# The adaptive-norm sums of two later stages: from one VectorE operation a step to a ScalarE multiply and a GpSimd add

## The chip, the cores and the metric

The kernel runs on one core of a Trainium2 chip. The metric is the device time of one launch in microseconds. "Before" was timed three times. All durations below that are not such a time come from one profiled execution.

## What is computed

Two transformer blocks stand one after the other, for 256 tokens of width 2048 in float32. The second block has two layers, each with adaptive modulation:

```python
c_act = jax.nn.silu(c)
for l in range(DEPTH_2):
    mod = c_act @ w_ada[l] + b_ada[l]                 # 2048 -> 3 * 2048
    shift, scale, gate = jnp.split(mod, 3, axis=-1)
    h = _rmsnorm(x, norm_g[l]) * (1.0 + scale[:, None, :]) + shift[:, None, :]
    z = h @ w_in[l]                                   # 2048 -> 13 pieces of 512
    ...                                               # four mixers
    y = jnp.concatenate([o_fft, o_na, o_ret, o_cv], axis=-1) @ w_out[l]
    x = x + gate[:, None, :] * y
```

The change is about `c_act @ w_ada[l]`: a product of one vector with 2 x 2048 x 6144 weights, 100 MB in all.

## The kernel before

**Blocks of the large products.** Every large weight matrix arrives in blocks of 128 x 2048 float32 (1 MB) in one of four rooms of `raw`. For each block ScalarE writes a float16 upper part (`w_hi`, L642), VectorE the float16 rest (`w_lo`, L1285), and TensorE does 48 matmuls of 256 columns (`product`, L2220). `w_hi` and `w_lo` have two slots each, so ScalarE can split block m only when TensorE has done block m-2, VectorE follows ScalarE, and TensorE starts block m when both are there and block m-1 is done. "Block m" is always the m-th of its stage. The stages of the second part are `z0` (52 blocks, from about 1251 us of the span to 1580), `mix0` (16 blocks, to about 1672), `z1` (52) and `mix1` (16).

**The modulation.** The sum `c_act @ w_ada` is cut into 12 units of 1024 outputs, and each unit into 16 steps, one for each chunk of 128 inputs. A step loads 128 x 1024 float32 of `w_ada` (0.5 MB) into one of two stage buffers (step n into buffer n % 2). VectorE multiplies it by a column of `SM` (one number a partition) and adds it to the unit's sum in one `scalar_tensor_tensor` (`ada_step`, L1256). The first step of a unit writes the sum with a `tensor_scalar` (L1253). When a unit is summed, ScalarE and VectorE split the sum in float16 parts (`ada_high`, `ada_low`), TensorE sums over the partitions (`ada_columns`, 16 matmuls of one column), and VectorE adds the bias (`ada_add`). Each of these waits for the one before it.

**What sets the order.** `ada_plan()` gives each step a stage and a block number. VectorE does the steps of block m right after its split of block m (`modulation`). The SyncE queue issues the loads: the steps of block m stand behind the weights of block m+2 (`load_due(2)`), and a step's load waits until its buffer is free, which is until step n-2 is done (`ada_used`). What stands behind a waiting load on that queue waits too. In `z0` and `z1` the old plan puts 32 steps (units 7, 8 and 10, 11) on blocks 2 to 29, three steps on two blocks up to block 10 and then one a block. In `mix0` it puts the 16 steps of unit 9 on blocks 2 to 11.

**Other VectorE work of `z0` and `z1`** stands behind the steps of its block: two `XT` updates a block (L1961) in the first blocks of `z0`, the gating of the convolution's input in block 10 (L1978, L1980), then 4 and more convolution taps a block (L1988, `TAPS_AT`) in blocks 11 to 38, and from block 20 on neighbourhood attention and rotation. GpSimd does nothing in these stages but one DMA a layer. In `mix0` VectorE adds gated results to `XT` (L2166).

Of the kernel before, what the change touches and what calls it, by code (L numbers as in the profile page):

```python
# [10 lines left out]
ALU = mybir.AluOpType  # L11
ACT = mybir.ActivationFunctionType
# [131 lines left out]
def ada_plan():  # L144

    at, count = {}, [0]

    def put(ph, m):
        at.setdefault(ph, {}).setdefault(m, []).append(count[0])
        count[0] += 1  # L150
    short = [2, 2, 3, 3, *range(4, 16)]
    def fast(ph):
        for m in [2 + 2 * k // 3 for k in range(13)] + list(range(11, 30)):
            put(ph, m)
    for m in [2 + 2 * k // 3 for k in range(16)]:
        put("w_in", m)
    for m in [3, 4, 4, 5, 6, 8, 10, 10, 12, 14, 15]:
        put("w_out", m)
    for m in [2, 2, 5, 5, 6, 6, 7, 8, 8, 10, 11, 14, 15]:
        put("wk", m)  # L160
    for ph in ("wq", "wv"):
        for k in range(26):
            put(ph, 16 * k // 26)
    for m in [0, 0, 1, 1, 2, 3, 4, 4, 5, 6, 6, 7, 8, 8, 9, 10, 10, 11, 12, 13]:
        put("wo", m)
    fast("z0")
    for m in [2, 2, 3, 4, 4, 5, 6, 6, 7, 8, 8, 9, 9, 10, 10, 11]:
        put("mix0", m)
    fast("z1")
    assert count[0] == 12 * ADA_STEPS  # L170
    return at


def ada_parts():

    names, out = {n: m for n, m, _ in STREAM}, {}
    following = {"wv": "wo"}
    for ph, steps in ada_plan().items():
        for m, ns in steps.items():
# [17 lines left out]
def build(nc, A, table, const_at, columns, router, out):  # L197
    ctx = ExitStack()
    with ctx:
# [174 lines left out]
        def ada_bank(u):  # L374
            return MB[:, 0, 0:8] if u in (8, 11) else GB[:, 2, 0:8]

# [177 lines left out]
        def _(gp):  # L554
# [64 lines left out]
        def _(act):  # L619
# [441 lines left out]
            for l in range(LAYERS):  # L1061
# [101 lines left out]
                for m in range(4 * PIECES):  # L1163
# [70 lines left out]
        def _(dve):  # L1234
# [23 lines left out]
            def ada_add(u):  # L1258
                dve.wait_ge(ada_mm, u + 1)
                mod = MOD[:, u // 6, u % 6 * 8:u % 6 * 8 + 8]  # L1260
                if u % 6 < 4:
# [4 lines left out]
            adds = {("w_in", 22): 0, ("wk", 10): 1, ("wq", 9): 2, ("wv", 3): 3, ("wv", 13): 4, ("wo", 8): 5,  # L1266
                    ("z0", 20): 7, ("z0", 33): 8, ("mix0", 14): 9, ("z1", 20): 10, ("z1", 33): 11}

# [30 lines left out]
            def modulation(ph, m):  # L1299
                if (ph, m) in parts_due:  # L1300
                    ada_low(parts_due[ph, m])
                for n in plan.get(ph, {}).get(m, []):
                    ada_step(n)
                if (ph, m) in adds:
# [660 lines left out]
            for l in range(LAYERS):  # L1965
# [202 lines left out]
                for m in range(2, 16):  # L2168
# [5 lines left out]
                    for p in nth(m, 6, 2, 5):  # L2174
                        pair_add(mix, p + 1)
                    if l == 0 and m == 14:
                        dve.wait_ge(ada_mod, 10)
# [22 lines left out]
        def _(pe):  # L2200
# [472 lines left out]
            for l in range(LAYERS):  # L2673
# [44 lines left out]
                def ret_scores(c):  # L2718
                    if c == 0:
                        pe.wait_ge(S("rotated"), 4 * l + 4)  # L2720
                        pe.wait_ge(S("na_max"), 8 * l + 8)
                        pe.wait_ge(ada_mod, 9 + 3 * l)
                    else:
# [100 lines left out]
                for m in range(4 * PIECES):  # L2824
                    if l == 0 and m == 3:
                        spread_root(3, r_first)
                    if m == 17:
                        ada_columns(7 + 3 * l)
                    if m == 32:
                        pe.wait_ge(S("na_max"), 8 * l + 8)  # L2830
                        ada_columns(8 + 3 * l)
# [31 lines left out]
                for m in range(16):  # L2863
                    if l == 0 and m == 13:
                        ada_columns(9)
# [107 lines left out]
```

## Time and profile before

| what | us |
|---|---|
| median of three runs (lowest, highest) | 2107.47 (2106.94, 2107.79) |
| time of the profiled execution | 2106.58 |
| its span | 2104.8 |
| TensorE busy in it | 2051.7 (97%) |
| VectorE busy | 1748.3 (83%) |
| ScalarE busy | 1195.1 (57%) |
| GpSimd busy | 41.3 (2%) |

The kernel is read as a row of stages in which TensorE hardly ever stops. The span less TensorE's busy time is 53 us, 28 us of it before 1251 us. What matters for a change in the later stages is where TensorE waits there and what it waits for.

### The profile page before, as it was taken

How to read it: one execution, taken by the hardware profiler on the slowest of the kernel's cores; microseconds unless marked ns; L12 is line 12 of the kernel's file. 1: busy time of each engine (PE TensorE's matmuls, PEld its weight loads, DVE VectorE, ACT ScalarE, POOL GpSimd, SP SyncE). 2: the span in 40 equal slices, each digit the busy share in tenths (PEclk: the TensorE clock that was granted, in tenths of full speed). 3: DMA queues.
4: the chain of work that ended last, by engine and by line, in shares of the span. 5: the costliest groups of instructions: out<-in, count | busy, mean ns of one | idle time of the engine just before them, and what ended most of it. 6: DMA issues, size and time to landing. Idle time of an engine off the chain costs nothing.

```text
span 2104.8 us, 42665 instructions
## 1 busy us (share of the span) xinstructions
PE 2051.7 (97%) x19032; PEld 1655.8 (79%) x19032; DVE 1748.3 (83%) x1660; ACT 1195.1 (57%) x1069; POOL 41.3 (2%) x40
## 2 busy tenths in 40 slices
PE   8999999999999999999999999999999999999998
PEld 7889888888889946555555568888888788888887
DVE  7885787988887798999999998999568789995655
ACT  5554644444434577887878864356554443565543
POOL 0002300000000000000000000000000000000000
PEclk9999999999999999999999999999999999999999
DMA  7854487788888878999999977874458778744552
GB/s 299 319 200 161 167 318 266 285 314 319 312 321 308 299 282 341 420 421 420 421 420 414 405 296 288 296 257 161 143 178 302 281 298 301 252 166 142 180 200 101
DMA packets 95718, 593.25 MB, mean 282 GB/s; under 512 B 10664, under 2 KB 10824, under 8 KB 36784
## 3 DMA queue, kind: packets, MB, share of 16 engines
q1 hardware_dynamic: 94912, 583.73, 74.0%
q0 software_dynamic: 624, 6.80, 0.8%
q8 instruction: 150, 2.46, 0.5%
q14 instruction: 32, 0.26, 0.0%
HBM read 588.39 MB, written 2.10 MB: 281 GB/s over the span
## 4 chain that ended last, share of the span: by engine, by line
PE 66%; DVE 17%; DMA 11%; ACT 3%; issue 3%; SPq 0%; DVEq 0%; POOL 0%; ACTq 0%; POOLq 0%
PE GB L2220 50%; DVE w_lo L1285 6%; DMA W<-w_ada 4%; PE GB L2646 4%; DVE W L1285 4%; PE MB L2646 3%; DMA Z<-w_ada 2%; ACT w_hi L642 2%; DMA raw<-w_down 2%; DVE W L1256 1%; DVE Z L1256 1%; DMA raw<-w_gate 1%; DMA raw<-w_up 1%; DMA Z<-w_up 1%; PE MB L2818 1%
## 5 line engine op out<-in xcount | busy, mean ns | idle before, releaser
L642 ACT ACTIVATE w_hi<-raw 128x2048 f16<-128x2048 f32 x294 | 561.2, 1910 | 710.4 <-PE GB L2220 687.8
L1285 DVE SCALAR_TENSOR_TENSOR w_lo<-raw,w_hi 128x2048 f16<-128x2048 f32 x294 | 674.1, 2294 | 245.9 <-ACT w_hi L642 244.8
L2220 PE MATMUL GB<-H,w_hi 128*128 128x256 f16 x4352 | 717.4, 273 | 18.2 <-DVE w_lo L1285 12.2
L2220 PE MATMUL GB<-H,w_lo 128*128 128x256 f16 x2176 | 593.2, 273 | 0.0
L2220 PEld LDWEIGHTS GB<-H,w_hi 128*128 128x128 f16 x4352 | 421.4, 98 | 84.0 <-DVE w_lo L1285 16.6
L2220 PEld LDWEIGHTS GB<-H,w_lo 128*128 128x128 f16 x2176 | 213.0, 98 | 24.7
L2220 PE MATMUL GB<-w_hi,H 128*128 128x256 f16 x1280 | 210.8, 273 | 0.9 <-DVE w_lo L1285 0.9
L1256 DVE SCALAR_TENSOR_TENSOR W<-W,SM 128x1024 f32<-128x1024 f32 x120 | 153.8, 1282 | 36.1 <-DMA W<-w_ada 32.8
L2220 PE MATMUL GB<-w_lo,H 128*128 128x256 f16 x640 | 174.4, 273 | 0.0
L2220 PE MATMUL GB<-Z,w_hi 128*128 128x256 f16 x1024 | 170.0, 274 | 3.6 <-DVE w_lo L1285 3.6
L2220 PE MATMUL GB<-W,w_hi 128*128 128x256 f16 x1024 | 168.0, 273 | 2.1 <-DVE w_lo L1285 2.1
L1285 DVE SCALAR_TENSOR_TENSOR W<-raw,W 128x2048 f16<-128x2048 f32 x68 | 154.4, 2286 | 3.4 <-ACT W L642 3.2
L642 ACT ACTIVATE W<-raw 128x2048 f16<-128x2048 f32 x68 | 129.6, 1912 | 30.4 <-PE GB L2646 8.1
L2220 PE MATMUL GB<-Z,w_lo 128*128 128x256 f16 x512 | 140.3, 274 | 0.0
L2220 PE MATMUL GB<-W,w_lo 128*128 128x256 f16 x512 | 139.6, 273 | 0.0
L2220 PEld LDWEIGHTS GB<-w_hi,H 128*128 128x128 f16 x1280 | 124.6, 98 | 17.4 <-DVE w_lo L1285 1.8
L2220 PEld LDWEIGHTS GB<-Z,w_hi 128*128 128x128 f16 x1024 | 100.3, 98 | 16.7 <-DVE w_lo L1285 4.5
L2220 PEld LDWEIGHTS GB<-W,w_hi 128*128 128x128 f16 x1024 | 99.9, 98 | 14.1 <-DVE w_lo L1285 2.6
L1988 DVE SCALAR_TENSOR_TENSOR Y<-Y,PC 128x256 f32<-128x256 f32 x240 | 99.6, 478 | 0.0
L2646 PE MATMUL MB<-W,Z 128*64 (+1 forms) x864 | 85.9, 353 | 3.5 <-DVE W L1285 2.0
L2646 PE MATMUL GB<-W,Z 128*64 (+1 forms) x864 | 86.5, 353 | 2.0 <-ACT Z L974 1.7
L2646 PE MATMUL GB<-w_hi,Z 128*64 (+1 forms) x576 | 84.8, 359 | 2.6 <-DVE Z L1858 1.5
(485 smaller groups left out, 2806.9 us busy)
## 6 DMA issues: line engine op xcount, KB each, us to landing
raw<-w_in SPq DMA_DIRECT2D x144, 1024.0 KB, 5.0
W<-w_ada SPq DMA_DIRECT2D x128, 512.0 KB, 5.6
raw<-w_out SPq DMA_DIRECT2D x48, 1024.0 KB, 5.2
raw<-w_down SPq DMA_DIRECT2D x41, 1024.0 KB, 10.7
raw<-w_gate SPq DMA_DIRECT2D x34, 1024.0 KB, 10.2
raw<-w_up SPq DMA_DIRECT2D x32, 1024.0 KB, 11.9
Z<-w_ada SPq DMA_DIRECT2D x64, 512.0 KB, 6.0
raw<-xattn_wk SPq DMA_DIRECT2D x16, 1024.0 KB, 5.2
```

What stands on the lines that cost most here:

```text
L642: act.activation(w, raw_at[r], ACT.Copy, scale=W_SCALE).then_inc(hi_done, 1)
L1256: dve.scalar_tensor_tensor(sums, w, SM[:, 24 + k:25 + k], sums, ALU.mult, ALU.add).then_inc(ada_used[n % 2], 1)
L1285: dve.scalar_tensor_tensor(lo, raw_at[r], W_SCALE, hi, ALU.mult, ALU.subtract).then_inc(raw_taken[r], 1)
L1988: dve.scalar_tensor_tensor(ca[:, c, :], CU[:, c, k // 4:k // 4 + T], col("conv_w_2", l * TAPS * 4 + k), ca[:, c, :], ALU.mult, ALU.add).th ...
L2220: last = pe.matmul(o, a, m, start=first, stop=end and w_part is lo, skip_group_check=True)
L2646: ins = pe.matmul(o_bank(j, k)[r:r + SLOT], x[:, c0 + c, at_:at_ + SLOT], v, start=kh == 0 and c == 0 and part == 0, stop=kh == 7 and c == ...
L2818: ins = pe.matmul(banks[:, n // 2, n % 2 * T:n % 2 * T + T], w[:, k, n * P:n * P + P], x[:, k, :], start=n % 2 == 0 and k == 0, stop=k == ...
```

## The change

The steps of `z0`, `mix0` and `z1` (80 of the 192) leave VectorE. ScalarE multiplies the arrived weights in place (`ada_scaled`), behind its split of the block and the copies out of PSUM; the first step of a unit writes the sum itself and needs no add. GpSimd adds the other 75 to the sum and frees the buffer (`ada_step` in the GpSimd program). The steps of `z0` and `z1` now stand on blocks 3 to 33: `3, 4, 4, 5, 6, ... 33`. Those of `mix0` stay on blocks 2 to 11, one of them a block later. The splits of the sums, the column sums and the bias adds move to later blocks to match, and the column sums of units 8 and 11 go to another PSUM bank.

```diff
+ON_GPSIMD = ("z0", "mix0", "z1")
-    def fast(ph):
-        for m in [2 + 2 * k // 3 for k in range(13)] + list(range(11, 30)):
+    def steady(ph):
+        for m in [3, 4] + list(range(4, 34)):
             put(ph, m)
-    for m in [2, 2, 3, 4, 4, 5, 6, 6, 7, 8, 8, 9, 9, 10, 10, 11]:
+    for m in [2, 2, 3, 4, 4, 5, 6, 6, 7, 8, 8, 9, 10, 10, 11, 11]:
         put("mix0", m)
...
+            def ada_step(n):
+                if n % ADA_STEPS == 0:
+                    return
+                gp.wait_ge(S("ada_scaled"), n - 7 * ADA_STEPS - (n // ADA_STEPS - 7))
+                gp.wait_ge(ada_used[(n - 1) % 2], (n - 1) // 2 + 1)
+                sums = ada_sums(n // ADA_STEPS)
+                gp.tensor_tensor(sums, sums, ada_stage(n), ALU.add).then_inc(ada_used[n % 2], 1)
...
+            def ada_scaled(ph, m):
+                for n in plan.get(ph, {}).get(m, []):
+                    u, k = n // ADA_STEPS, n % ADA_STEPS
+                    act.wait_ge(ada_full[n % 2], 16 * (n // 2 + 1))
+                    c, w = SM[:, 24 + k:25 + k], ada_stage(n)
+                    if k:
+                        act.activation(w, w, ACT.Copy, scale=c).then_inc(S("ada_scaled"), 1)
+                        continue
+                    act.wait_ge(ada_mm, u - 1)
+                    act.activation(ada_sums(u), w, ACT.Copy, scale=c).then_inc(ada_used[n % 2], 1)
...
-                    ("z0", 20): 7, ("z0", 33): 8, ("mix0", 14): 9, ("z1", 20): 10, ("z1", 33): 11}
+                    ("z0", 24): 7, ("z0", 40): 8, ("mix0", 15): 9, ("z1", 24): 10, ("z1", 40): 11}
...
-                for n in plan.get(ph, {}).get(m, []):
-                    ada_step(n)
+                if ph not in ON_GPSIMD:
+                    for n in plan.get(ph, {}).get(m, []):
+                        ada_step(n)
...
-                        pe.wait_ge(ada_mod, 9 + 3 * l)
...
                 def conv_sum(k, src, o):
                     if k == 0:
+                        pe.wait_ge(ada_mod, 9 + 3 * l)
...
-                    if m == 17:
+                    if m == 22:
                         ada_columns(7 + 3 * l)
-                    if m == 32:
-                        pe.wait_ge(S("na_max"), 8 * l + 8)
+                    if m == 37:
+                        pe.wait_ge(S("rotated"), 4 * l + 4)
                         ada_columns(8 + 3 * l)
```

On VectorE, in blocks 11 to 13 of `z0`, the steps stand between the split and the taps before:

```order
L1285 SCALAR_TENSOR_TENSOR w_lo<-raw,w_hi 128x2048 [waits hi_done]
L1256 SCALAR_TENSOR_TENSOR Z<-Z,SM 128x1024 [waits ada_used1,ada_full0]
L1988 SCALAR_TENSOR_TENSOR Y<-Y,PC 128x256 [waits tap] x4
L1285 SCALAR_TENSOR_TENSOR w_lo<-raw,w_hi 128x2048 [waits hi_done]
L1256 SCALAR_TENSOR_TENSOR Z<-Z,SM 128x1024 [waits ada_used0,ada_full1]
L1988 SCALAR_TENSOR_TENSOR Y<-Y,PC 128x256 [waits tap] x4
```

Now, with line numbers of the changed kernel, only split and taps are left:

```order
L1312 SCALAR_TENSOR_TENSOR w_lo<-raw,w_hi 128x2048 [waits hi_done]
L2016 SCALAR_TENSOR_TENSOR Y<-Y,PC 128x256 [waits tap] x4
L1312 SCALAR_TENSOR_TENSOR w_lo<-raw,w_hi 128x2048 [waits hi_done]
L2016 SCALAR_TENSOR_TENSOR Y<-Y,PC 128x256 [waits tap] x4
L1312 SCALAR_TENSOR_TENSOR w_lo<-raw,w_hi 128x2048 [waits hi_done]
```

One VectorE operation of each block is gone, and with it VectorE's wait for the arrival of `w_ada`.

On ScalarE, in blocks 4 to 7 of `mix0`, there were splits (L642) and the squares of a pair of `XT` chunks (L932):

```order
L642 ACTIVATE w_hi<-raw 128x2048 [waits block_done0,raw_full2]
L932 ACTIVATE Z<-XT 128x512 [waits bank_free0]
L642 ACTIVATE w_hi<-raw 128x2048 [waits block_done1,raw_full3]
L642 ACTIVATE w_hi<-raw 128x2048 [waits block_done0,raw_full0]
L932 ACTIVATE Z<-XT 128x512 [waits bank_free1]
L642 ACTIVATE w_hi<-raw 128x2048 [waits block_done1,raw_full1]
```

Now the multiplies (L672) stand between them, each with its wait for the load (`ada_full`):

```order
L655 ACTIVATE w_hi<-raw 128x2048 [waits block_done0,raw_full2]
L672 ACTIVATE W<-W,SM 128x1024 [waits ada_full1]
L672 ACTIVATE W<-W,SM 128x1024 [waits ada_full0]
L956 ACTIVATE Z<-XT 128x512 [waits bank_free0]
L655 ACTIVATE w_hi<-raw 128x2048 [waits block_done1,raw_full3]
L672 ACTIVATE W<-W,SM 128x1024 [waits ada_full1]
L655 ACTIVATE w_hi<-raw 128x2048 [waits block_done0,raw_full0]
L672 ACTIVATE W<-W,SM 128x1024 [waits ada_full0]
L672 ACTIVATE W<-W,SM 128x1024 [waits ada_full1]
```

Six multiplies moved in front of the splits of blocks 5 to 8, and the wait for `w_ada` came with them.

## Rows read from the trace of the kernel before

**Rows 1.** Page, part 1: busy us (share of the span) and instructions.

```profile
PE 2051.7 (97%) x19032; PEld 1655.8 (79%) x19032; DVE 1748.3 (83%) x1660; ACT 1195.1 (57%) x1069; POOL 41.3 (2%) x40
```

**Rows 2.** Windows: stretch, us, then busy us (instructions) of each engine, clock, DMA.

```profile
1268.00:1345.00 77.00, 73.00 (x660) 63.98 (x658) 71.12 (x80) 32.15 (x23) 0.00 (x0) 1.00 0.85 309
1345.00:1543.00 198.00, 196.70 (x1715) 165.38 (x1714) 167.48 (x216) 113.22 (x142) 0.00 (x0) 1.00 0.57 196
...
1625.00:1672.00 47.00, 44.76 (x420) 39.44 (x418) 35.39 (x33) 20.36 (x16) 0.00 (x0) 1.00 0.73 261
1695.00:1738.00 43.00, 42.19 (x387) 37.58 (x386) 34.29 (x26) 19.11 (x14) 0.00 (x0) 1.00 0.95 360
1738.00:1783.00 45.00, 43.85 (x415) 39.12 (x413) 44.17 (x53) 18.17 (x13) 0.00 (x0) 1.00 0.84 298
1783.00:1872.00 89.00, 88.23 (x784) 74.26 (x783) 88.28 (x130) 53.94 (x84) 0.00 (x0) 1.00 0.63 220
```

**Rows 3.** Waits of TensorE in mix0 and z0: start, length, operation, [idle before].

```profile
1638.49 0.39 PE L2220 MATMUL GB<-W,w_hi 128*128 128x256 f16 x2 [1.20 <-DVE w_lo L1285]
...
1318.74 0.39 PE L2220 MATMUL GB<-H,w_hi 128*128 128x256 f16 x2 [1.40 <-DVE w_lo L1285]
```

**Rows 4.** Timeline of VectorE in z1, blocks 10 to 13.

```profile
1734.72 1.28 DVE L1256 SCALAR_TENSOR_TENSOR Z<-Z,SM 128x1024 f32<-128x1024 f32 x1 [1.12 <-DMA Z<-w_ada]
...
1737.26 1.38 DVE L1980 TENSOR_SCALAR Y<-Y,PC 128x256 f32<-128x256 f32 x4
...
1743.54 2.29 DVE L1285 SCALAR_TENSOR_TENSOR w_lo<-raw,w_hi 128x2048 f16<-128x2048 f32 x1
1745.74 1.28 DVE L1256 SCALAR_TENSOR_TENSOR Z<-Z,SM 128x1024 f32<-128x1024 f32 x1
1746.94 1.67 DVE L1988 SCALAR_TENSOR_TENSOR Y<-Y,PC 128x256 f32<-128x256 f32 x4
1748.52 2.28 DVE L1285 SCALAR_TENSOR_TENSOR w_lo<-raw,w_hi 128x2048 f16<-128x2048 f32 x1
```

**Rows 5.** Timeline of ScalarE in z1 and mix0.

```profile
1746.41 1.91 ACT L642 ACTIVATE w_hi<-raw 128x2048 f16<-128x2048 f32 x1 [4.65 <-PE GB L2220]
...
1751.65 1.91 ACT L642 ACTIVATE w_hi<-raw 128x2048 f16<-128x2048 f32 x1 [2.85 <-PE GB L2220]
...
1646.01 1.06 ACT L651 ACTIVATE ada_hi<-W 128x1024 f16<-128x1024 f32 x1
```

**Rows 6.** Timeline of GpSimd from 188 us, where it works beside VectorE.

```profile
188.38 1.88 POOL L580 TENSOR_TENSOR Z<-Z 128x1020 f32<-128x1020 f32 x1
...
192.37 1.44 POOL L591 TENSOR_TENSOR Y<-Z 128x512 f32<-128x512 f32 x1
...
214.25 3.92 POOL L580 TENSOR_TENSOR Y<-Z 128x1016 f32<-128x1016 f32 x1
```

**Rows 7.** Timeline of VectorE in the same stretch.

```profile
188.48 2.07 DVE L1511 TENSOR_TENSOR Z<-Z,RT 128x256 f32<-128x256 f32 x1
...
191.93 0.41 DVE L1511 TENSOR_TENSOR Z<-Z,RT 128x256 f32<-128x256 f32 x1
...
192.60 3.35 DVE L1285 SCALAR_TENSOR_TENSOR w_lo<-raw,w_hi 128x2048 f16<-128x2048 f32 x1
...
214.16 2.28 DVE L1285 SCALAR_TENSOR_TENSOR w_lo<-raw,w_hi 128x2048 f16<-128x2048 f32 x1
```

**Rows 8.** Timelines of VectorE and GpSimd at the end of the span.

```profile
2096.53 3.55 DVE L2196 TENSOR_TENSOR Z<-XT,MB 128x1024 f32<-128x1024 f32 x4 [1.29 <-PE MB L2272]
...
2097.36 2.35 POOL L615 TENSOR_TENSOR Z<-XT,NS 128x1024 f32<-128x1024 f32 x1 [422.18 <-ACT NS L1230]
```

**Rows 9.** DMA issues from 1590 to 1650 us, and of the page: KB, median us to landing.

```profile
W<-w_ada SPq DMA_DIRECT2D x14, 512.0 KB, 4.8
...
Z<-w_ada SPq DMA_DIRECT2D x64, 512.0 KB, 6.0
```

**Rows 10.** Chain that ended last, a piece of z1: start, us, what.

```profile
1721.17 3.92 DMA Z<-w_ada
```

More of the change, by code:

```diff
@@ L165, in ada_plan @@
         put("wo", m)
-    fast("z0")
-    for m in [2, 2, 3, 4, 4, 5, 6, 6, 7, 8, 8, 9, 9, 10, 10, 11]:
+    steady("z0")
+    for m in [2, 2, 3, 4, 4, 5, 6, 6, 7, 8, 8, 9, 10, 10, 11, 11]:
         put("mix0", m)
-    fast("z1")
+    steady("z1")
     assert count[0] == 12 * ADA_STEPS
@@ L181, in ada_parts @@
                 if n % ADA_STEPS == ADA_STEPS - 1:
+                    m += ph in ON_GPSIMD
                     out[(ph, m + 1) if m + 1 < names[ph] else (following[ph], 0)] = n // ADA_STEPS
@@ L374, in ada_bank @@
         def ada_bank(u):
-            return MB[:, 0, 0:8] if u in (8, 11) else GB[:, 2, 0:8]
+            return GB[:, 2, 0:8]
         def na_p(h):
@@ L613, in _ @@
                 gp.dma_start(W[:, 0:2 * BLK], A["na_rel_bias_2"][l]).then_inc(S("bias_in"), 16)
+                for ph in (f"z{l}", f"mix{l}"):
+                    for n in [n for m in sorted(plan.get(ph, {})) for n in plan[ph][m]]:
+                        ada_step(n)
             gp.wait_ge(S("final_x"), 8)
@@ L1169, in _ @@
                         evict(i, 1)
+                    if m >= 3:
+                        ada_scaled(ph, m)
                     for c in nth(m, 22, 3):
@@ L1213, in _ @@
                     split(mix, m)
+                    ada_scaled(mix, m)
                     for p in nth(m, 4, 2, 6):
@@ L1301, in modulation @@
                     ada_low(parts_due[ph, m])
-                for n in plan.get(ph, {}).get(m, []):
-                    ada_step(n)
+                if ph not in ON_GPSIMD:
+                    for n in plan.get(ph, {}).get(m, []):
+                        ada_step(n)
                 if (ph, m) in adds:
@@ L2175, in _ @@
                         pair_add(mix, p + 1)
-                    if l == 0 and m == 14:
+                    if l == 0 and m == 15:
                         dve.wait_ge(ada_mod, 10)
@@ L2863, in _ @@
                 for m in range(16):
-                    if l == 0 and m == 13:
+                    if l == 0 and m == 14:
                         ada_columns(9)
```

## The prediction

> **What bounds the kernel now.** I read the page's busy shares first: TensorE is busy 97% of the span and VectorE 83% [rows 1]. A change off TensorE can only give back TensorE's waits, or add to them. So the second view is the windows over the stages that the change touches [rows 2]: TensorE idles 4.00 us of 1268 to 1345 and 1.30 of 1345 to 1543 (z0), 2.24 of 1625 to 1672 (mix0), and 0.81, 1.15 and 0.77 of the three stretches of z1. That is 10.3 us, of which some 0.9 (short gaps at small products) are not VectorE's. **At most 9.4 us can be won**, 0.45% of the time. The third view is what TensorE waits for: VectorE's split `w_lo`, 1.40 us in z0 and 1.20 in mix0 at the longest [rows 3].
>
> The fourth is how full VectorE is. In blocks 11 to 19 of z1 it is busy 44.17 of 45 us, in blocks 20 to 33 88.28 of 89 [rows 2], while TensorE hardly waits: **VectorE stands exactly at the edge there**. One block is split 2.20 (start to start), step 1.20, taps 1.58, together 4.98 us [rows 4], against 5.24 between ScalarE's splits, which is TensorE's pace (1746.41 to 1751.65) [rows 5]. The slack inside a block is 5.24 less ScalarE's 1.91, VectorE's 2.29 and handovers of 0.1, so 0.9 us.
>
> **The parts of the change: VectorE.** It sheds 75 steps of 1.20 and 5 shorter ones. What matters is how its other operations get on beside GpSimd's adds. Beside GpSimd's add of 1.88 us a VectorE operation of 0.41 took 2.07, so it stood for 1.66; a split of 2.29 took 3.35 beside an add that had begun 0.23 earlier and ended 1.21 after the split's start; and the other way round an add of the same kind took 3.92 where a split of 2.28 had begun first [rows 6, 7]. **The two exclude each other for nearly the whole instruction.** A rate shared in halves would have given other numbers. The exception is also in the trace: four VectorE operations with one operand in PSUM took 3.55 us, 1024 + 1024 + 512 + 512 columns at the usual rate, while GpSimd worked [rows 8]. The split, the taps and the rotation have both inputs in SBUF; the `XT` updates and the masks of attention have one in PSUM.
>
> A rule that speaks against the change is in the Trainium skill, "GPSIMD Engine Reference", section "Engine selection": elementwise adds belong on VectorE. The Trainium skill's same page, section "Elementwise — side-by-side cycle accounting", has 4497 ns for an add of 2048 columns on GpSimd, from which I estimate 2.25 us for 1024. The trace has 1.88 us for 1020 columns [rows 6]; by the Trainium skill's figure the sum would be some 5 to 10 us larger, which is near rival (c).
>
> So a step costs VectorE 0 before the add and up to 1.75 us with it (1.88 less its last 0.13 to 0.15, in which VectorE already ran: 1.06 of 1.21), in place of 1.20. **Bounds of a step for VectorE: -1.20 (the add falls wholly beside idle or PSUM work) to +0.55 (it falls beside nothing of the kind).**
>
> Blocks 11 to 19 of z have nothing but splits and taps: 3.78 + 1.75 = 5.53, with the lost overlap of two starts 5.6 us against 5.24. That is 0.36 for each of 9 blocks, 3.2 us. Block 10 holds the gating, 2.5 us between the end of its step and the next split, and its step waits 1.12 us for the load [rows 4]. It goes to 2.2 + 2.5 + 1.75 = 6.45 of 5.24, and the 1.2 above it less the slack of 0.9 cost 0.4. Together 3.6. Against the 1.15 us that z1 loses there now [rows 2], this is **+2.4**; in z0, which loses 1.40 there [rows 3], **+2.2**.
>
> Blocks 20 to 33: VectorE's 88.28 us less ten steps (12.0) and a split of the sums that moves on to block 35 (1.1) is 75.1. Fourteen adds bring 24.5, so 99.6, of which four adds can lie beside the attention's masks and maxima (7.0) and some beside copies out of PSUM (3.1): 89.5 against 89. I take +0.5 for this, +0.5 for ScalarE below, each in z0 and z1; bounds -0.8 and +10.
>
> The first blocks of z: VectorE no longer waits for loads ahead of a split. Of the 2.6 us lost there in z0 (4.00 - 1.40) and 0.8 in z1, 0.8 stays in z0 (block 5 waits for its load on ScalarE, and the next split comes late). **-1.8 and -0.8.**
>
> **ScalarE** gets 80 multiplies of about 1.0 us (the nearest row is 1.06 for 1024 columns with another output type [rows 5]). Cover: it waits 2.85 us before a split in block 12 [rows 5], and is busy 53.94 of 89 us in blocks 20 to 33 [rows 2]; with 14 us more, 68 of 89. Only block 22 with its exponentials overruns. What it costs when the cover is gone: everything behind a late multiply on ScalarE, which is the next split, and so TensorE.
>
> **The loads in mix0** are the largest term. A buffer goes round like this: load 4.8 us [rows 9], multiply 1.0, add 1.9, handovers 0.1, so 7.8; with two buffers 3.9 us a step. Before it was 4.8 + 1.28, so 3.05 a step. The plan wants 16 steps in blocks 2 to 11, 1.6 a block, so 3.3 us a step. Before, the ring just held and lost 2.1 us; now a block cannot be faster than 1.6 x 3.9 = 6.2 us. Walking it block by block (split, multiplies as their loads land, next split not before them; adds behind VectorE's splits, 2.25 us at most) gives waits of TensorE of 1.5, 2.2, 2.0, 2.0 and 2.1 at blocks 5, 7, 9, 11 and 12, together 9.8. **+7.7.** With landings of 3.9, the shortest on the chain that ended last [rows 10], seven rounds give back 6.3; with 6.0, the median over z0 and z1 [rows 9], they cost 8.4 more: **bounds +1.4 and +16**. I take 4.8, since it is the row of this stage. On SyncE's queue the weight loads stand behind those of the steps; they are issued three blocks ahead, which covers waits of 2 us.
>
> In z with one step a block the ring has 10.5 us a round and needs 6.0 + 1.0 + 1.9 and up to 2.3 behind a split, 11.2 at worst: ScalarE waits some tenths, in cover. TensorE's waits on the column sums and biases come 3 and more blocks after the last step: nothing.
>
> **Sum.** z0: -1.8 + 2.2 + 1.0 = +1.4. z1: -0.8 + 2.4 + 1.0 = +2.6. mix0: +7.7. Together +11.7 on a span of 2104.8: 2116.5. The profiled execution was 1.8 us above its span and 0.9 below the median, so the median comes to **2119.2 us**.
>
> **Rivals.** (a) Faster, 2101.5: the exclusion decides. If VectorE's splits and taps are not held up by adds (GpSimd gives way, or its adds fall into VectorE's idle time, as the operations of 0.41 beside GpSimd's one-input work did (at 191.93) [rows 7]), all of z's waits of 7.3 us (4.6 and 2.7) come back; with landings of 3.9 mix0 costs 1.4, together -5.9. It decides at 0.26 us of held time a block, VectorE's room in blocks 11 to 19. Against it: rows 6 and 7. (b) No change, 2107 to 2111: one of the two mechanisms is absent. With no exclusion and the ring as walked: -7.3 + 7.7, 2108. With landings of 3.9 and half of z's 4.0: +3.4, 2111. (c) Worse, 2135: the add takes 2.35 us as the only one of 1024 columns did [rows 8], which is 0.47 x 23 blocks x 2 in z less some overlap (+14), and 3 us in mix0; ScalarE then waits for loads in blocks 20 to 33 with little cover. (d) The steps of mix0 are not spread by the change; a reader of its title would expect them to be. That is in the sum.
>
> **How the numbers follow.** Forecast 0.48, (c) 0.19, (b) 0.18, (a) 0.15. A measurement can tell about 0.2%, 4.2 us. Slower is the forecast, (c) and 0.03 of (b): 0.70. Within 0.2% is the rest of (b) and 0.02 of (a): 0.17. Faster: 0.13. The range leaves out (a) and the far end of (c): 2103 to 2137.
>
> **What would show it.** Right: TensorE's idle time in mix0 near 10 us with ScalarE's next split late behind a wait for `w_ada`; splits of VectorE of 3 to 4 us in blocks 11 to 33; VectorE still some 95% busy in z1's blocks 11 to 19. Wrong: splits of 2.29 throughout, adds under 1.5 us, or landings under 4 us in mix0. If the splits are long and TensorE doesn't wait, then the room in blocks 11 to 33 was larger than I read it.

## The result and the profile after

The changed kernel takes 2147.61 us (median of four runs, 2144.84 to 2150.33) against 2107.20 of the kernel before in the same comparison: ratio 1.0191, interval 1.0178 to 1.0205, so 40.4 us slower. The forecast was 12 us slower with a range up to 2137. The sign was right, the size was a third of what came, and the time lies outside the range.

The profiled execution is the longest of the four: 2150.33 us, span 2148.5, so 43.7 more than the span before (2104.8). What its stages show is therefore some 3 us more than the medians do.

Busy time of the engines, to be read beside [rows 1]:

```profile
PE 2063.3 (96%) x19032; PEld 1659.3 (77%) x19032; DVE 1749.0 (81%) x1580; ACT 1279.1 (60%) x1149; POOL 268.8 (13%) x115
```

Two lines tell most of the story. VectorE has 80 instructions less, and is busy as long as before (1749.0 against 1748.3). TensorE does the same 19032 matmuls in 11.6 us more, and idles 32.1 us more (2148.5 less 2063.3 against 2104.8 less 2051.7).

The stages, cut at the starts of ScalarE's splits of blocks 3, 11, 20 and 34 of `z0`, 0 of `mix0`, 2, 11, 20 and 34 of `z1`, and 0 of `mix1`. The windows view of the changed kernel (columns as in [rows 2]):

```profile
1266.10:1309.80 43.70, 42.07 (x382) 37.15 (x381) 27.70 (x29) 28.32 (x23) 21.15 (x8) 1.00 0.81 291
1309.80:1365.70 55.90, 49.41 (x435) 42.73 (x433) 52.20 (x49) 30.08 (x25) 25.59 (x9) 0.97 0.73 260
1365.70:1461.00 95.30, 90.46 (x783) 74.98 (x781) 93.34 (x112) 67.36 (x98) 50.74 (x15) 0.98 0.64 227
1461.00:1593.20 132.20, 128.27 (x1084) 108.77 (x1084) 89.88 (x91) 66.92 (x66) 0.00 (x0) 1.00 0.47 160
1593.20:1708.70 115.50, 103.87 (x917) 90.16 (x915) 73.03 (x79) 65.47 (x63) 38.44 (x16) 0.97 0.75 269
1708.70:1758.20 49.50, 47.45 (x434) 42.04 (x433) 28.05 (x22) 31.75 (x28) 21.33 (x8) 1.00 0.73 265
1758.20:1811.90 53.70, 47.68 (x435) 41.97 (x433) 52.21 (x47) 30.26 (x24) 27.37 (x9) 1.00 0.75 266
1811.90:1914.00 102.10, 92.74 (x784) 75.76 (x781) 100.99 (x116) 67.84 (x98) 41.77 (x15) 0.97 0.60 212
1914.00:2044.80 130.80, 128.17 (x1084) 108.68 (x1084) 88.65 (x89) 66.89 (x66) 1.58 (x1) 1.00 0.47 162
```

And of the kernel before, blocks 20 to 33 of `z0` and of `z1`, cut in the same way:

```profile
1362.00:1450.80 88.80, 88.23 (x782) 74.18 (x781) 88.15 (x129) 53.95 (x85) 0.00 (x0) 1.00 0.63 221
1783.50:1872.50 89.00, 88.23 (x783) 74.21 (x781) 88.28 (x131) 53.96 (x85) 0.00 (x0) 1.00 0.63 220
```

The lengths beside those of before, and beside four of the kernels below, each cut in the same way from its own trace (us):

| stage | before | after | predicted more | came more | step_on_vector | add_on_vector | tail_on_vector | mix0_alone |
|---|---|---|---|---|---|---|---|---|
| z0, blocks 3 to 10 | 44.1 | 43.7 | -1.8 | -0.4 | 41.8 | 42.5 | 41.7 | 41.7 |
| z0, 11 to 19 | 50.2 | 55.9 | +2.2 | +5.7 | 48.7 | 48.6 | 48.7 | 48.7 |
| z0, 20 to 33 | 88.8 | 95.3 | +1.0 | +6.5 | 90.2 | 89.4 | 88.4 | 88.4 |
| z0, 34 to the end | 129.0 | 132.2 | 0 | +3.2 | 133.0 | 132.9 | 130.2 | 130.2 |
| mix0 to block 2 of z1 | 106.7 | 115.5 | +7.7 | +8.8 | 107.6 | 111.2 | 107.2 | 114.0 |
| z1, 2 to 10 | 48.1 | 49.5 | -0.8 | +1.4 | 47.1 | 48.0 | 47.1 | 47.2 |
| z1, 11 to 19 | 48.9 | 53.7 | +2.4 | +4.8 | 47.3 | 47.2 | 47.3 | 47.3 |
| z1, 20 to 33 | 89.0 | 102.1 | +1.0 | +13.1 | 90.5 | 89.6 | 88.4 | 88.3 |
| z1, 34 to the end | 129.0 | 130.8 | 0 | +1.8 | 131.3 | 131.2 | 130.2 | 130.2 |

The parts of `z0` are 15.0 us longer, `mix0` 8.8, the parts of `z1` 21.1.

**Where VectorE's gain went.** The groups of VectorE's taps and splits, of GpSimd's adds and of ScalarE's multiplies, as in part 5 of the page (busy us, mean ns of one | idle before):

```profile
L2016 DVE SCALAR_TENSOR_TENSOR Y<-Y,PC 128x256 f32<-128x256 f32 x240 | 170.8, 772 | 0.0
L1312 DVE SCALAR_TENSOR_TENSOR w_lo<-raw,w_hi 128x2048 f16<-128x2048 f32 x294 | 683.8, 2327 | 306.0 <-ACT w_hi L655 304.7 <-DVE Y L2016 0.3
L578 POOL TENSOR_TENSOR Z<-Z 128x1024 f32<-128x1024 f32 x60 | 189.5, 3159 | 243.9 <-ACT Z L672 243.6
L578 POOL TENSOR_TENSOR W<-W 128x1024 f32<-128x1024 f32 x15 | 37.9, 2525 | 171.3 <-ACT W L672 171.2
L672 ACT ACTIVATE Z<-Z,SM 128x1024 f32<-128x1024 f32 x60 | 68.4, 1140 | 11.7 <-DMA Z<-w_ada 11.6
```

Before, the 294 splits were busy 674.1 us, and the 240 taps:

```profile
L1988 DVE SCALAR_TENSOR_TENSOR Y<-Y,PC 128x256 f32<-128x256 f32 x240 | 99.6, 478 | 0.0
```

So the taps alone took back 71.2 us and the splits 9.7. A timeline of VectorE in blocks 11 and on of `z0`:

```profile
1316.58 4.97 DVE L2016 SCALAR_TENSOR_TENSOR Y<-Y,PC 128x256 f32<-128x256 f32 x4
1321.48 2.28 DVE L1312 SCALAR_TENSOR_TENSOR w_lo<-raw,w_hi 128x2048 f16<-128x2048 f32 x1
1323.68 3.78 DVE L2016 SCALAR_TENSOR_TENSOR Y<-Y,PC 128x256 f32<-128x256 f32 x4
1327.38 2.28 DVE L1312 SCALAR_TENSOR_TENSOR w_lo<-raw,w_hi 128x2048 f16<-128x2048 f32 x1
1329.59 1.66 DVE L2016 SCALAR_TENSOR_TENSOR Y<-Y,PC 128x256 f32<-128x256 f32 x4
...
1344.53 2.27 DVE L1312 SCALAR_TENSOR_TENSOR w_lo<-raw,w_hi 128x2048 f16<-128x2048 f32 x1
1346.73 5.91 DVE L2016 SCALAR_TENSOR_TENSOR Y<-Y,PC 128x256 f32<-128x256 f32 x4
1352.57 2.28 DVE L1312 SCALAR_TENSOR_TENSOR w_lo<-raw,w_hi 128x2048 f16<-128x2048 f32 x1
```

And GpSimd's in the same stretch:

```profile
1324.84 2.34 POOL L578 TENSOR_TENSOR Z<-Z 128x1024 f32<-128x1024 f32 x1 [3.96 <-ACT Z L672]
...
1344.30 4.73 POOL L578 TENSOR_TENSOR Z<-Z 128x1024 f32<-128x1024 f32 x1 [1.17 <-ACT Z L672]
1350.02 2.35 POOL L578 TENSOR_TENSOR Z<-Z 128x1024 f32<-128x1024 f32 x1 [0.99 <-ACT Z L672]
```

Four taps take 1.66 us without an add, 3.78 with one (2.12 more, of an add of 2.34), and 5.91 where two adds fall on them. The first of the two had begun beside the split and itself took 4.73. A block with one add goes from split to split in 5.90 us (1321.48 to 1327.38), where TensorE needs 5.24. With two adds it is 8.04 (1344.53 to 1352.57), and the short blocks beside it can give back little, since the weights' parts have two slots only. The hold fell on the taps and hardly on the splits (mean 2327 ns, 2294 before), so the prediction's sign for it, splits of 3 to 4 us, was the wrong place to look.

**What some waits cost on top.** Timeline of TensorE at the same place:

```profile
1323.81 0.61 PE L2248 MATMUL GB<-H,w_hi 128*128 128x256 f16 x2 [2.58 <-DVE w_lo L1312]
```

The windows view ahead of its start and behind it:

```profile
1320.00:1324.00 4.00, 1.42 (x13) 0.99 (x11) 4.00 (x4) 2.67 (x3) 0.88 (x1) 0.93 0.38 140
1324.00:1327.00 3.00, 3.00 (x16) 2.17 (x15) 3.00 (x4) 0.76 (x1) 2.16 (x1) 0.52 0.70 238
1327.00:1330.50 3.50, 3.50 (x34) 3.14 (x33) 3.50 (x5) 0.00 (x0) 0.18 (x1) 1.00 0.60 246
```

Behind a wait of 2.58 us the granted clock is 0.52, the lower level of 1.2 GHz, and TensorE does 16 matmuls in 3.00 us in place of about 30. Not every wait is followed by this. The same kernel's wait of 2.63 us that ends at 1354.9 is not:

```profile
1354.00:1358.00 4.00, 3.09 (x29) 2.78 (x30) 4.00 (x6) 1.32 (x2) 0.00 (x0) 1.00 0.55 150
```

Of its seven waits of 2 us or more in these nine stages two are followed by the lower clock, and so are three of 1.77 to 1.97 us. Over the span the mean granted clock is 0.987 against 0.992. That is 2148.5 x 0.013 less 2104.8 x 0.008, 11.1 us, beside the 11.6 us by which the same matmuls were busy longer. Not all of it belongs to the change: in the nine stages TensorE is busy 10.1 us longer, and the clocks and lengths of their windows give some 8 us.

**mix0.** ScalarE ahead of its split of block 7 of `mix0`, with its waits for the loads:

```profile
1629.90 1.15 ACT L672 ACTIVATE W<-W,SM 128x1024 f32<-128x1024 f32 x1 [2.60 <-DMA W<-w_ada]
1633.38 1.15 ACT L672 ACTIVATE W<-W,SM 128x1024 f32<-128x1024 f32 x1 [2.33 <-DMA W<-w_ada]
1634.44 0.61 ACT L956 ACTIVATE Z<-XT 128x512 f32<-128x512 f32 x1
1634.96 1.89 ACT L655 ACTIVATE w_hi<-raw 128x2048 f16<-128x2048 f32 x1
```

TensorE's longest wait there:

```profile
1639.78 0.39 PE L2248 MATMUL GB<-W,w_hi 128*128 128x256 f16 x2 [3.79 <-DVE w_lo L1312]
```

The split comes late behind two waits for `w_ada`, as the walk had it. A hold adds to it: an operation of VectorE that takes 0.68 us alone takes 2.43 beside GpSimd's add, and VectorE begins its split 0.6 us after ScalarE has done its own:

```profile
1635.08 2.43 DVE L1365 TENSOR_TENSOR Z<-Z 128x512 f32<-128x512 f32 x1 [5.00 <-ACT Z L956]
```

### The profile page after: what moved, and what is told of

Its sections match the earlier page's. It is cut to its first block, busy times and chain, and to the rows that moved or that the text cites. A ratio compares the mean times of both kernels' runs of the same rounds, so it can differ in the third digit from the quotient of the medians.

```text
span 2148.5 us, 42741 instructions
## 1 busy us (share of the span) xinstructions
PE 2063.3 (96%) x19032; PEld 1659.3 (77%) x19032; DVE 1749.0 (81%) x1580; ACT 1279.1 (60%) x1149; POOL 268.8 (13%) x115
## 3 DMA queue, kind: packets, MB, share of 16 engines
q8 instruction: 150, 2.46, 0.4%
## 4 chain that ended last, share of the span: by engine, by line
PE 52%; DVE 20%; issue 13%; DMA 8%; ACT 5%; POOL 1%; POOLq 0%; ACTq 0%; SPq 0%; DVEq 0%
PE GB L2248 38%; DVE w_lo L1312 8%; PE GB L2674 4%; DVE Y L2016 4%; DVE W L1312 3%; PE MB L2674 3%; ACT w_hi L655 3%; DMA W<-w_ada 3%; DMA raw<-w_up 2%; DMA raw<-w_down 1%; POOL W L578 1%; DMA raw<-w_gate 1%; DMA Z<-w_up 1%; DMA Z<-w_down 1%; DVE W L1283 1%
## 5 line engine op out<-in xcount | busy, mean ns | idle before, releaser
L1312 DVE SCALAR_TENSOR_TENSOR w_lo<-raw,w_hi 128x2048 f16<-128x2048 f32 x294 | 683.8, 2327 | 306.0 <-ACT w_hi L655 304.7
L2248 PE MATMUL GB<-H,w_hi 128*128 128x256 f16 x4352 | 725.1, 274 | 30.9 <-DVE w_lo L1312 26.2
L578 POOL TENSOR_TENSOR Z<-Z 128x1024 f32<-128x1024 f32 x60 | 189.5, 3159 | 243.9 <-ACT Z L672 243.6
L2016 DVE SCALAR_TENSOR_TENSOR Y<-Y,PC 128x256 f32<-128x256 f32 x240 | 170.8, 772 | 0.0
L1283 DVE SCALAR_TENSOR_TENSOR W<-W,SM 128x1024 f32<-128x1024 f32 x105 | 134.6, 1282 | 19.9 <-DMA W<-w_ada 16.8
```

The lines of the kernel that those rows point to most:

```text
L578: gp.tensor_tensor(sums, sums, ada_stage(n), ALU.add).then_inc(ada_used[n % 2], 1)
L1283: dve.scalar_tensor_tensor(sums, w, SM[:, 24 + k:25 + k], sums, ALU.mult, ALU.add).then_inc(ada_used[n % 2], 1)
L1312: dve.scalar_tensor_tensor(lo, raw_at[r], W_SCALE, hi, ALU.mult, ALU.subtract).then_inc(raw_taken[r], 1)
L2016: dve.scalar_tensor_tensor(ca[:, c, :], CU[:, c, k // 4:k // 4 + T], col("conv_w_2", l * TAPS * 4 + k), ca[:, c, :], ALU.mult, ALU.add).th ...
L2248: last = pe.matmul(o, a, m, start=first, stop=end and w_part is lo, skip_group_check=True)
```

## The experiments

The theory before the runs, H: VectorE stands still while GpSimd adds, and this is what costs in `z0` and `z1`. Rivals: S, that the cost is the extra ScalarE work and the longer use of the two stage buffers; P, that it is the new plan of blocks. Beside the kernels before and after, ten more stand in the table. "z" is the sum of the eight stages of `z0` and `z1` above, "mix0" that stage, "taps" the mean ns of one of the 240 taps. The kernel before was 2107.20 us in the comparison of the changed kernel, 2105.18 in that of the next eight and 2106.61 in that of the last two. Three of the expectations below (tail_on_vector, tail_on_gpsimd, mix0_alone) count stages from cuts one or two blocks earlier: there `mix0` is 102.4 us before, 111.3 after and 102.8 in tail_on_vector, and what the change adds behind the cut near block 34 is 9 us in both layers (5.0 in the table above).

| kernel | median us (lowest, highest) | ratio [interval] | z | mix0 | taps |
|---|---|---|---|---|---|
| before | | | 627.1 | 106.7 | 478 |
| after | 2147.61 (2144.84, 2150.33) | 1.0191 [1.0178, 1.0205] | 663.2 | 115.5 | 772 |
| add_on_vector | 2115.04 (2109.99, 2121.14) | 1.0046 [1.0029, 1.0063] | 629.4 | 111.2 | 477 |
| step_on_vector | 2109.12 (2106.83, 2115.88) | 1.0019 [1.0004, 1.0034] | 629.9 | 107.6 | 476 |
| add_64_columns | 2096.90 (2092.00, 2101.15) | 0.9954 [0.9934, 0.9973] | 619.1 | 107.4 | 482 |
| add_512_columns | 2103.84 (2101.79, 2105.86) | 0.9993 [0.9980, 1.0006] | 619.3 | 110.9 | 584 |
| one_input | 2108.71 (one run) | | 623.2 | 115.5 | 558 |
| mix0_back | 2136.01 (2132.51, 2139.37) | 1.0139 [1.0112, 1.0165] | 659.0 | 109.2 | 749 |
| tail_on_vector | 2100.95 (2098.56, 2105.97) | 0.9979 [0.9965, 0.9992] | 622.0 | 107.2 | 479 |
| tail_on_gpsimd | 2144.80 (2135.01, 2148.72) | 1.0196 [1.0166, 1.0226] | 647.6 | 115.1 | 730 |
| mix0_alone | 2109.31 (2106.21, 2113.35) | 1.0014 [1.0002, 1.0027] | 622.0 | 114.0 | 482 |
| add_in_quarters | 2148.16 (2145.45, 2152.23) | 1.0211 [1.0191, 1.0231] | 647.0 | 128.0 | 696 |

### add_on_vector: is it that GpSimd adds?

```diff
-                for ph in (f"z{l}", f"mix{l}"):
-                    for n in [n for m in sorted(plan.get(ph, {})) for n in plan[ph][m]]:
-                        ada_step(n)
...
+            def ada_sum(n):
...
+                dve.tensor_tensor(sums, sums, ada_stage(n), ALU.add).then_inc(ada_used[n % 2], 1)
...
-                if ph not in ON_GPSIMD:
-                    for n in plan.get(ph, {}).get(m, []):
-                        ada_step(n)
+                for n in plan.get(ph, {}).get(m, []):
+                    (ada_sum if ph in ON_GPSIMD else ada_step)(n)
```

> The multiply stays on ScalarE, the add of the 75 steps goes from GpSimd to VectorE (a tensor_tensor of some 1.2 us in the step's old place); plan and column sums as in the changed kernel. Theory H (GpSimd's add of 2.34 us holds VectorE's operations with two inputs in SBUF): no hold is left, VectorE needs 4.9 us a block as before, so the 36 us that z0 and z1 lost go; what stays is the longer ring of mix0 (4.8 + 1.1 + 1.2 = 7.1 us a round, 5.7 a block: +3 to +5), so 2107 to 2114. Theory S (ScalarE's multiply with its wait for the load makes the next split late): nothing changes there, 2135 or more.

1.0046, where the changed kernel is 1.0191: 1.45% or some 30 us go with GpSimd alone, though VectorE now does 75 adds more. The groups of VectorE's taps and of its new adds:

```profile
L2020 DVE SCALAR_TENSOR_TENSOR Y<-Y,PC 128x256 f32<-128x256 f32 x240 | 99.5, 477 | 0.0
L1288 DVE TENSOR_TENSOR Z<-Z 128x1024 f32<-128x1024 f32 x60 | 73.1, 1218 | 3.4 <-ACT Z L669 3.1
```

The taps are back at 477 ns with all of ScalarE's multiplies in place. An add that takes VectorE 1.22 us as its own work took it 2.12 as GpSimd's. The time, 2115.04 us, is 1 us above the range that H gave and 20 under that of S. H holds for z (629.4 us against 663.2), and S is excluded there.

### add_64_columns and add_512_columns: by length

```diff
-                gp.tensor_tensor(sums, sums, ada_stage(n), ALU.add).then_inc(ada_used[n % 2], 1)
+                gp.tensor_tensor(sums[:, 0:64], sums[:, 0:64], ada_stage(n)[:, 0:64], ALU.add).then_inc(ada_used[n % 2], 1)
```

> GpSimd adds only the first 64 of the 1024 columns of each step, so the sums of units 7 to 11 leave out most of their terms; multiplies, loads and waits are all there. Theory H: the hold shrinks from 2.3 to some 0.3 us a step, VectorE is rid of 1.2 us a step, and the ring of mix0 is down to 6.3 us a round: 2099 to 2105, faster than before. Theory S: 2135 or more.

> GpSimd adds half of each step's columns (the other half of each sum is left out), 1.27 us by the rows of 512 columns. Theory H: what the hold takes (1.1 us) is what VectorE was rid of (1.2), so the loss is not half of the way between 64 and 1024 columns (2122) but most of it is gone: 2103 to 2113. If every held microsecond costs TensorE the same, 2120 or more.

With 64 columns z is 619.1 us, 8.0 under before and 44.1 under after, and the time is 2 us below the range given. With 512 columns z is 619.3, so half an add costs nothing at all over one of 64 columns, and a whole one 43.9 us. The timeline of VectorE in two blocks of `z0` with 512 columns shows why:

```profile
1325.64 2.68 DVE L2016 SCALAR_TENSOR_TENSOR Y<-Y,PC 128x256 f32<-128x256 f32 x4
1328.68 2.29 DVE L1312 SCALAR_TENSOR_TENSOR w_lo<-raw,w_hi 128x2048 f16<-128x2048 f32 x1 [0.35 <-ACT w_hi L655]
1330.89 2.68 DVE L2016 SCALAR_TENSOR_TENSOR Y<-Y,PC 128x256 f32<-128x256 f32 x4
```

The hold is there, 1.02 us for an add of 1.35 (2.68 less 1.66), but 2.20 + 2.68 is 4.9 of TensorE's 5.24, and VectorE still waits 0.35. With 2.12 it is 5.90. **The price of a hold is what stands out of the block's slack**, here 1.46 us by this sum: a hold of 1.02 was free, one of 2.12 was not.

### one_input: does a GpSimd operation that reads one operand hold VectorE?

```diff
-                gp.tensor_tensor(sums, sums, ada_stage(n), ALU.add).then_inc(ada_used[n % 2], 1)
+                gp.tensor_scalar(sums, ada_stage(n), 1.0, None, ALU.mult).then_inc(ada_used[n % 2], 1)
```

> GpSimd copies the scaled weights over the sum with a tensor_scalar of 1024 columns instead of adding them, so each sum holds its last step alone. Question: does an operation with one input of the same size hold VectorE as the add does? If each operation of GpSimd that reads SBUF holds the pair for its whole length (some 3 us by the row of 1.49 us for 512 columns), 2150 or more. If it holds it only while it reads, less than the add: under 2130.

z is 623.2, under before; what is lost is in `mix0`. The timeline of VectorE beside such a copy in `z0`:

```profile
1334.93 2.44 DVE L2016 SCALAR_TENSOR_TENSOR Y<-Y,PC 128x256 f32<-128x256 f32 x4
```

And that of GpSimd at the same time:

```profile
1335.89 2.94 POOL L578 TENSOR_SCALAR Z<-Z 128x1024 f32<-128x1024 f32 x1 [3.49 <-ACT Z L672]
```

GpSimd is busy longer than with the add (2.94 against 2.34 at the shortest) and the taps are held 0.78 us only. VectorE's next split starts at 1337.96, while the copy still runs, and takes its usual 2.29. So it is not GpSimd's being busy that holds VectorE. The copy differs from the add in its second operand and in its kind of instruction; that the operand makes the difference is likely, and not shown apart. It is a single run; the blocks before and behind this one show the same 2.44.

### add_in_quarters: one long hold or four short ones

```diff
-                gp.tensor_tensor(sums, sums, ada_stage(n), ALU.add).then_inc(ada_used[n % 2], 1)
+                for q in range(4):
+                    cut = slice(256 * q, 256 * q + 256)
+                    ins = gp.tensor_tensor(sums[:, cut], sums[:, cut], ada_stage(n)[:, cut], ALU.add)
+                ins.then_inc(ada_used[n % 2], 1)
```

> The changed kernel with each GpSimd add of 1024 columns cut into four of 256 columns; the sums are the same. Theory T (VectorE stands still for as long as GpSimd's two-input work takes in all, however it is cut): VectorE's four taps of blocks 11 to 19 are still 3.5 to 6 us, and the time is 2143 to 2155. Theory L (a hold lasts for one instruction and VectorE gets in between two; an add of 512 columns cost nothing, so what costs is one long hold that the block's slack can't take): VectorE and GpSimd take turns, the taps beside an add take about 1.7 + 2.4 us at the most since the total is the same, but the split of ScalarE's next block is met by shorter holds, and the time is 2120 to 2143. Theory S (a short instruction hardly holds VectorE at all, its reading being the only exclusive part): the taps take under 2.5 us beside the quarters and the time is 2104 to 2115.

The time fits theory T's number and most of the reason is not T's. z falls by 16.2 us (663.2 to 647.0), and most groups of four taps take 3.3 to 3.6 us beside the quarters, where a whole add made 3.8 of them, so VectorE does get in between two instructions, as theory L had it. In blocks 11 to 19 it is held as long in all as with whole adds (busy 52.1 and 51.2 us against 52.2 and 52.2), in blocks 20 to 33 less (90.0 and 92.0 against 93.3 and 101.0). But the four instructions of a step take GpSimd longer (61.1 us for the 60 in `mix0`, 4.1 a step against 2.5), and `mix0` goes from 115.5 to 128.0. The time alone would have misled; the stages tell it.

### step_on_vector and tail_on_vector: what the new plan does

step_on_vector is the changed kernel with whole steps on VectorE, as before, but at the new blocks; ScalarE's multiplies and GpSimd's adds are gone.

```diff
...
-                if ph not in ON_GPSIMD:
-                    for n in plan.get(ph, {}).get(m, []):
-                        ada_step(n)
+                for n in plan.get(ph, {}).get(m, []):
+                    ada_step(n)
```

> Whole steps back on VectorE (the fused operation of 1.28 us), but at the new places of the plan and with the moved column sums. Theory H and theory S: 2103 to 2109, since neither the hold nor the multiply is left. Theory P (the new plan itself costs, through four more steps in the full blocks 30 to 33 and the later column sums): 2112 or more.

1.0019, and 2109.12 us, at the upper edge of the range of H and S; the 2112 or more of P did not come. The stages are worth more than the sum: the steadier plan gains 3.8 and 2.6 us up to block 20 of the two stages and loses 5.4 and 3.8 behind it, 4.0 and 2.3 of them behind block 34. TensorE at block 34 of `z0` in this kernel:

```profile
1461.61 1.14 PE L2747 MATMUL MB<-Z 64*128 64x256 f32 x8 [2.74 <-DVE Z L2044]
1462.68 0.39 PE L2241 MATMUL GB<-H,w_hi 128*128 128x256 f16 x2
...
1463.03 0.63 PE L2241 MATMUL GB<-H,w_hi 128*128 128x256 f16 x2
```

The windows view of the wait and of what follows it:

```profile
1459.00:1462.70 3.70, 1.09 (x9) 0.71 (x10) 3.63 (x7) 3.31 (x3) 0.00 (x0) 1.00 0.70 213
1463.00:1466.00 3.00, 3.00 (x16) 2.13 (x15) 3.00 (x4) 2.20 (x3) 0.00 (x0) 0.50 0.13 52
```

The retention scores wait 2.74 us for VectorE's rotation (before it does not wait for it), because steps on blocks 30 to 33 stand ahead of it on VectorE, and behind the wait the clock is 0.50 for 3 us. In `z1` the same product waits 2.74 us too, and the clock behind it stays at 1.00:

```profile
1887.00:1892.00 5.00, 4.96 (x44) 4.18 (x45) 5.00 (x7) 3.02 (x5) 0.00 (x0) 1.00 0.35 146
```

In the changed kernel the same product waits 1.55 us in `z0` and 1.75 in `z1`. With adds of 64 or 512 columns at the same blocks the product doesn't wait (under 0.5 us). So I moved the last four steps behind the rotation, and the column sums from block 37 to 39 (`mix0` has its old plan again):

```diff
-        for m in [3, 4] + list(range(4, 34)):
+        for m in [3, 4] + list(range(4, 30)) + [34, 35, 36, 37]:
...
-                    if m == 37:
+                    if m == 39:
```

> Steps on VectorE as before the change, mix0 as before. In z0 and z1 the steps stand on blocks 3, 4, 4, 5, ... 29 and 34 to 37, so one a block, but not on blocks 30 to 33, where the rotation for TensorE's products of block 34 is made; the second column sum comes at block 39. Theory R (the 4 us that step_on_vector lost at block 34 of each layer come from VectorE's late rotation): the gain of the even first blocks (4.7 us in step_on_vector's stages) stays and the loss goes, 2099 to 2103 where before is 2105. If the loss at block 34 is of the later column sums, it stays: 2108 or more.

2100.95, ratio 0.9979 [0.9965, 0.9992]: **faster than the kernel before** by 4.2 us, with the change's plan mended and no step on GpSimd. The same product waits 0.74 us, and the loss behind block 20 is down to 0.8 and 0.6 us. The column sums come later here than in step_on_vector, so they did not make its loss.

> The changed kernel (multiply on ScalarE, add on GpSimd) with the same placing, nothing on blocks 30 to 33 but four steps on 34 to 37. Theory R for the part that TensorE loses after block 33 (9 us in both layers) and theory H for the rest: 2136 to 2142. By theory H alone, with the number of adds what counts and not their place: 2146 or more.

The same plan with GpSimd's adds gave 1.0196, beside 1.0191 of the changed kernel. The time doesn't tell the two expectations apart; the runs spread over 14 us, and the profiled one is the shortest. Its blocks 20 to 33 are 2.8 and 7.4 us shorter than those of the changed kernel, with four adds fewer in them, and what follows 0.8 and 0.7. Whether this is a gain in the median stays open.

### mix0_back and mix0_alone: the two stage buffers

mix0_back takes only `mix0` back to VectorE and the old plan; mix0_alone is tail_on_vector with only `mix0` as in the change.

The line that differs in mix0_back, and the same line in mix0_alone:

```diff
-ON_GPSIMD = ("z0", "mix0", "z1")
+ON_GPSIMD = ("z0", "z1")
...
-ON_GPSIMD = ("z0", "mix0", "z1")
+ON_GPSIMD = ("mix0",)
```

> The 16 steps of mix0 stand on VectorE again with the old plan for them; z0 and z1 as in the changed kernel. If the three stages add up, what mix0 lost (8.7 us of the stage's length) comes back: 2138 to 2140. If mix0's loss was made in z0 (late splits carried over), less than 4 us come back.

> z0 and z1 as in tail_on_vector (whole steps on VectorE, none on blocks 30 to 33), and only the 16 steps of mix0 as in the change: multiplied by ScalarE, added by GpSimd, with the change's plan for mix0. Theory A (the loss in mix0 is that of the two stage buffers, which are taken longer by a multiply and an add, and is independent of z0 and z1): the stage of mix0 up to block 2 of z1 is 111 us as in the change (102.8 in tail_on_vector), all other stages are within 0.5 us of tail_on_vector, and the time is 2100.95 + 8.5, so 2107 to 2111. Rival B (much of that loss in the change is work that z0 left late, or needs adds in z1): the stage is under 107 us and the time under 2105.

Taken away, the change in `mix0` gives back 6.3 us of its stage and 0.5% of the time (1.0191 to 1.0139). Done alone, it costs 6.8 us of its stage and 0.35% (0.9979 to 1.0014), and z stays at 622.0. So most of the 8.8 us is independent of the holds in z; some 2 us come only with them. The first came out 2 us below its range and the second 1.5 us under the changed kernel's stage, which theory A had it reach; its time is in A's range.

The column "mix0" over all kernels is a second test. A buffer is taken for the load, and then for a step of: 1.28 us whole on VectorE (106.7 to 107.6, and 109.2 in mix0_back), 1.15 + 0.46 with 64 columns (107.4), 1.15 + 1.22 with the add on VectorE (111.2), 1.15 + 1.35 with 512 columns (110.9), 1.15 + 2.53 in the change (115.5), 1.15 + 2.90 with one input (115.5), 1.15 + 4.1 in quarters (128.0). The stage grows with this time, whichever engine does the step.

## Why the prediction was wrong, step by step

**The bound on what could be won, 9.4 us: right.** With the holds nearly gone (add_64_columns) z is 8.0 us shorter than before, where TensorE's waits in z had been put at 7.3, and the median 8.3.

Two small readings of the prediction are off, without effect on the sum: the wait of 2.85 us stands before ScalarE's split of block 14, not 12, and 1.2 less 0.9 is 0.3 for block 10.

**"A step costs VectorE up to 1.75 us (1.88 less its last 0.13 to 0.15)": the mechanism was right, the term was mis-sized.** The add takes 2.34 us and holds 2.12. I took the 1.88 of [rows 6], an add of a tile to a shifted view of it; the only add of two operands of 1024 columns in the trace was the 2.35 of [rows 8], which I priced as rival (c). The estimate from the Trainium skill, "GPSIMD Engine Reference", section "Elementwise — side-by-side cycle accounting", 2.25 us, was nearer than my row; the measured number is 2.34. The difference of 0.37 is small for an add, but it is all above the slack: in blocks 11 to 19 the same sum with 2.12 is 3.78 + 2.12 = 5.90 a block, 53.1 us for nine, and 53.7 came in `z1`. In `z0` 55.9 came. There block 10's gating was held, one block had two adds on its taps, and the clock was at the lower level for 3 us. With 1.75 it was 5.6, or 50.4.

**"Blocks 20 to 33: 89.5 against 89, so +0.5" (and 0.5 for ScalarE): the step that failed most**, with +6.5 and +13.1 us. Fourteen adds at 2.12 in place of 1.75 are 5.2 us of it. With them the forecast of VectorE's busy time, 1.2 us more than before, becomes 6.4 more. In `z0` 5.2 more came (93.34 against 88.15), so there the cover of 10.1 us, adds beside operations with an input in PSUM, was about right. In `z1` 12.7 more came (100.99 against 88.28), so some 6 us of that cover were not there: the same fourteen adds fell on taps. Why they fell so in one layer and not in the other the runs don't show; mix0_back has it too (92.2 and 101.9 us). The other 1.3 and 0.4 us are idle time of VectorE itself, which the sum took as none. TensorE at the lower clock, for 3 us in `z0` and twice that in `z1`, is part of these lengths too. ScalarE had room (67.36 of 95.30), as predicted.

**"Waits on column sums and biases: nothing": true of these, but the wrong wait was asked.** The steps on blocks 30 to 33 delay the rotation, and with it TensorE's scores at block 34. The stages from block 34 on are 3.2 and 1.8 us longer in the change, 4.0 and 2.3 in step_on_vector, where GpSimd adds nothing, and 1.2 each once the four steps stand behind it. I had costed the move of the steps by VectorE's total, not by who waits for the operation behind them.

**First blocks, -1.8 and -0.8: wrong, -0.4 and +1.4.** With whole steps on VectorE at the new blocks the gain was there (-2.3 and -1.0), with ScalarE's multiplies and the adds on VectorE it was -1.6 and -0.1. I had costed no hold beside the `XT` updates and the gating; a `TENSOR_TENSOR` of the gating took 2.46 us in the change and 1.16 in the two kernels without GpSimd.

**mix0, +7.7: the place and the mechanism right, the number helped by luck.** +8.8 came. TensorE waited 0.78, 3.79, 2.12 and 2.07 us in it, 8.8 together, where the walk had 9.8 in five waits. But a round of a buffer was longer than I took it: landings of 4.7 us (4.8 taken), multiplies of 1.15 (1.0) and adds of 2.53 (1.9), 0.7 us more. By the walk's own rule, 6.3 us for 0.9 a round, that is 5 us on top of 7.7. They did not come, and done alone the change in `mix0` cost 6.8. What made up for them is open.

**No term for the clock: missing.** Some 8 of the 44 us of the profiled execution are matmuls at the lower clock behind waits. I had costed each wait at its own length.

**Together:** in z the forecast was +4.0 and +36.1 came, 17.6 of the difference in blocks 20 to 33. Rival (c) had the right price for the add (2.35) and 28 us in all; it lacked the rotation, the clock and the missing cover in `z1`. I gave it 0.19 because I took the size of the add from the row whose engine neighbourhood was best, and not from the row whose shape was the same. My range ended at 2137 since it left the far end of (c) out; with my own bounds of +10 for blocks 20 to 33 of each stage and +16 for `mix0` the sum reaches 2146, which is still under what came.

## What to carry to other kernels

Moving a two-input SBUF operation from VectorE to GpSimd doesn't free VectorE where its neighbours read two SBUF operands: price it at nearly GpSimd's own duration (here 2.12 us held of 2.34, in place of 1.22 on VectorE), and count only what stands above the slack of a block, since below it such an add is free. Don't count on cover from other work beside it unless the order makes it sure: of the same fourteen adds one layer had some 11 us covered and the other 4. When steps move in a program with an order written by hand, ask of each new place which waited-for operation now stands behind it; that, not the engine's total, cost here 4 us a stage and, mended, made the faster kernel. Some waits of TensorE of about 2 us and more were followed by 3 us at half speed and others of the same length were not; over the changed stages this was 8 us of 45, which belongs in the price.

## What the runs showed of the hardware that I had not expected

- The one-input operation held VectorE much less than the add. The Trainium skill, "SBUF — State Buffer", section "Who interferes with whom", says that a VectorE instruction with two SBUF inputs contends with a GpSimd instruction that reads SBUF, and calls the port pair that the two share an exclusive lock. For the two-input add the trace agrees (2.12 of 2.34 us). For the one-input operation it agrees in part only: of 2.94 us the taps were held 0.78, and a split beside its end not at all.
- GpSimd's adds of 64, 512 and 1024 columns took 0.46, 1.35 and 2.53 us on average in `mix0`, and 1.02, 2.16 and 3.16 in `z0` and `z1`, beside a full VectorE. Even 64 columns took GpSimd half a microsecond more there.
- Cut in four, the same add held most groups of four taps 1.7 to 1.9 us in place of 2.12, sometimes a split by 0.5 besides, and took GpSimd 4.1 us in place of 2.5.
- The lower clock came in stretches of some 3 us behind waits of 1.8 to 3.8 us, and not behind others of 2.60 and 2.74 us.
